# Half-size expert weight chunks, router logits taken from x, and output transposes laid between the last scatter products

## The chip, the cores and the metric

The kernel runs on one core of a Trainium2 chip, in float32. The metric is device time in microseconds (us) of one execution. Three executions of the kernel before took 1821.88, 1827.37 and 1827.48 us; the median is 1827.37 us. A separate profiled execution took 1822.55 us, and the span from its first to its last instruction was 1820.4 us.

## The reference

One inference step of a two-layer decoder for 256 prompt tokens and 8 sample tokens (264 in all, D = 1024). Each layer has a mixer, then a feed-forward part. The change lies wholly in the feed-forward part of layer 1, a top-2-of-8 mixture of experts:

```
h = rms_norm(x, norm_ffn)                       # x * rsqrt(mean(x*x)) * w
logits = einsum('btd,de->bte', h, moe_router)   # 8 experts
probs = softmax(logits); top_p, top_i = top_k(probs, 2); top_p /= sum(top_p)
hg = einsum('btd,edf->btef', h, moe_w_gate)     # F = 1792
hu = einsum('btd,edf->btef', h, moe_w_up)
a  = silu(hg) * hu * gate
x  = x + einsum('btef,efd->btd', a, moe_w_down)
```

## The kernel before

Activations lie transposed, `x[:, d, :]` being 128 features by 264 tokens, for d from 0 to 7. Each engine runs its own program; semaphores order them. SyncE (SP) issues all weight loads on one queue.

**The weights of the experts.** They are cut into 42 sets: two groups g of four experts, and 21 sets t for each group. Sets 0 to 13 hold pieces of the gate and up matrices (`GU_SETS`: 4 row blocks k by 512 columns, or in the last two 8 row blocks by 256 columns), sets 14 to 20 two row blocks of the down matrix. A set is four transfers of 1024 KB, one for each expert, so all are 168 transfers. Three sets fit on the chip at a time (set t lies in slots 4*(t%3) to 4*(t%3)+3). `load_set(n)` waits until `sets_used` says that set n-3 is used up and then issues its four transfers. Sets 1, 2 and 0 are loaded ahead, during the end of the mixer.

**The router** (`route`). After the last output product of the mixer (`wo`, d = 7) ScalarE squares x, TensorE sums the squares in PSUM bank 0, ScalarE forms `rs` (logarithm, then exponential), and VectorE's `xnorm` writes h = x * w * rs in eight steps. TensorE multiplies h by the router matrix (L1481), again into bank 0, VectorE copies the logits, TensorE turns them so that tokens are rows, and a chain of small VectorE steps finds the two experts of each token (`top`), the counts (`r_flag`) and the slot matrix G (`r_slots`). Meanwhile TensorE turns h itself to rows (`token_rows`) and ScalarE copies it to `htok`.

**The gather** (`gather_first`). Six products of no use (`WARM_R`) run once the branch is taken; then four `gather_pair` calls multiply `htok` by G, and ScalarE copies the results to `hs`, the tokens of each expert side by side.

**Hidden and down products** (`hidden_chosen`, `down_chosen`). For each set TensorE waits until all of it has landed, then works for r = 0 and 1 (32 products each, four of them side by side in the array, columns 32j) and in between two `over_piece` calls of 16 for experts with many tokens, whose weights VectorE copies out first (`bring`, L2853). The sets of gate and up are followed by `turn_hidden`. `sets_used` is raised at the first product of the next set.

**The end.** The sums of the down products lie in banks 0, 1, 4, 5 and 6; ScalarE copies them to `ys`. `scatter(1, d)` multiplies them back to tokens, for eight d, in banks 4 + d % 4; VectorE adds each to x (`add_tile`, L2823). When all are added, `give_back` turns x to rows (24 transposes in banks 0 to 5), and ScalarE copies the banks and issues the three output transfers.

## Time and profile before

| | us |
|---|---|
| median of three executions | 1827.37 |
| profiled execution | 1822.55 |
| its span | 1820.4 |
| TensorE busy | 1757.7 (97% of the span) |
| VectorE busy | 746.4 (41%) |
| ScalarE busy | 362.3 (20%) |
| first expert product; copy of the last down sum begins | 1362.61; 1800.81 |

TensorE's busy time is the time in which some product is under way; it says little on whether a product waited for anything else. Times below count from the span's start.

### The profile page before, as it was taken

The page shows a single profiled execution, that of the slowest core. Times are in us where ns is not written, and L with a number is a line of the kernel's source. Part 1 is how long each engine was busy: PE and PEld are TensorE (multiplying, and loading weights), DVE is VectorE, ACT ScalarE, POOL GpSimd, SP SyncE. Part 2 cuts the span into 40 slices and gives each one's busy share as a digit, 9 for nine tenths or more (in the row PEclk, how much of TensorE's full clock was granted, in tenths as well). Part 3 has the DMA queues.
Part 4 walks back from the last instruction along what each step waited for, and adds up shares of the span by engine and source line. Part 5 has one row for each costly group of instructions (what it writes and reads, how often), then busy time and mean ns, then how long its engine had stood idle before and what let it go on. Part 6 is the DMA issues. An engine that isn't in the chain of part 4 may idle for free.

```text
span 1820.4 us, 30085 instructions
## 1 busy us (share of the span) xinstructions
PE 1757.7 (97%) x12545; PEld 1299.3 (71%) x12545; DVE 746.4 (41%) x1551; ACT 362.3 (20%) x760; POOL 154.3 (8%) x259
## 2 busy tenths in 40 slices
...
GB/s 289 286 120 104 194 308 342 349 327 365 387 341 395 357 324 272 303 354 362 159 85 262 285 350 342 314 370 380 341 91 320 393 379 414 385 397 393 380 414 157
DMA packets 263163, 563.94 MB, mean 310 GB/s; under 512 B 11965, under 2 KB 160673, under 8 KB 262752
## 3 DMA queue, kind: packets, MB, share of 16 engines
...
## 4 chain that ended last, share of the span: by engine, by line
PE 86%; DMA 7%; SPq 3%; DVE 2%; issue 1%; ACT 1%; POOL 0%; DVEq 0%; ACTq 0%
PE PS L930 34%; PE PS L1364 8%; PE PS L1585 7%; PE PS L1340 5%; PE PS L1372 4%; PE PS L849 3%; SPq L801 3%; PE PS L1623 3%; DMA mem<-in_moe_w_up 3%; PE PS L976 3%; PE PS L1565 3%; PE PS L1354 2%; DMA z<-in_moe_w_down 2%; PE PS L969 2%; PE PS L1524 2%; PE PS L1311 1%
## 5 line engine op out<-in xcount | busy, mean ns | idle before, releaser
L930 PE MATMUL PS<-h,mem 128*128 128x264 f32 x2816 | 655.4, 389 | 0.0
L930 PEld LDWEIGHTS PS<-h,mem 128*128 128x128 f32 x2816 | 528.6, 191 | 107.0 <-issue 21.3
L1773 ACT COPY z<-PS 128x264 f32<-128x264 f32 (+6 forms) x311 | 127.5, 430 | 817.0 <-PE PS L930 528.2
L1585 PE MATMUL PS<-mem,z 128*32 128x512 f32 (+1 forms) x1536 | 148.8, 533 | 15.9 <-DMA mem<-in_moe_w_up 9.0
L1585 PEld LDWEIGHTS PS<-mem,z 128*32 128x32 f32 x1536 | 54.6, 112 | 87.5 <-issue 78.1
L2853 DVE COPY small<-mem 128x1024 f32 x56 | 38.9, 694 | 170.4 <-PE PS L1565 112.7
L1565 PE MATMUL PS<-small,z 128*32 128x256 f32 (+2 forms) x624 | 87.8, 396 | 0.0
L1340 PE MATMUL PS<-z,mem 128*128 128x264 f32 x384 | 87.3, 388 | 0.0
L1565 PE MATMUL PS<-z 128*32 128x256 f32 (+2 forms) x624 | 87.1, 397 | 0.0
L1340 PEld LDWEIGHTS PS<-z,mem 128*128 128x128 f32 x384 | 72.3, 190 | 13.8 <-issue 1.7
L1364 PE MATMUL PS<-z,mem 128*128 128x132 f32 x624 | 78.3, 278 | 0.0
L1364 PEld LDWEIGHTS PS<-z,mem 128*128 128x128 f32 x624 | 74.5, 192 | 0.0
L1565 PEld LDWEIGHTS PS<-small,z 128*32 128x32 f32 x624 | 37.0, 110 | 48.6 <-issue 40.5
L1770 ACT ACTIVATE z<-z 128x1056 f32<-128x1056 f32 (+3 forms) x54 | 56.9, 1053 | 62.3 <-DVEq L2677 54.2
L1364 PE MATMUL PS<-h,mem 128*128 128x132 f32 x488 | 63.2, 278 | 2.8 <-DVE h L2174 2.8
L1372 PE MATMUL PS<-z,mem 128*128 128x132 f32 x550 | 63.5, 276 | 0.0
L1623 PE MATMUL PS<-mem,z 128*32 128x512 f32 x512 | 58.1, 593 | 5.0 <-DMA mem<-in_moe_w_down 5.0
L1372 PEld LDWEIGHTS PS<-z,mem 128*128 128x128 f32 x550 | 62.6, 190 | 0.0
L1364 PEld LDWEIGHTS PS<-h,mem 128*128 128x128 f32 x488 | 59.2, 192 | 3.2 <-issue 3.2
L1354 PE MATMUL PS<-z,mem 128*128 128x264 f32 x256 | 59.5, 387 | 2.0 <-DVE z L2612 2.0
L1770 ACT ACTIVATE z<-x 128x264 f32<-128x264 f32 x32 | 13.1, 421 | 235.1 <-DVE x L2619 160.2
L1585 PE MATMUL PS<-z 128*32 128x512 f32 x512 | 58.0, 593 | 1.2 <-DMA z<-in_moe_w_up 1.2
...
## 6 DMA issues: line engine op xcount, KB each, us to landing
out_win_s<-in_cache_win_kv SPq DMA_DIRECT2D x128, 1023.5 KB, 11.7
...
```

Of the source, the lines that this page charges most:

```text
L801: sp.dma_start(v3(slot_ap(s_), src.shape[1]), src).then_inc(landed[s_], 16)
L849: return tr(out, in_, ident[0:rows, 0:rows])
L930: last = mm(bank(l, "p", j)[:, 0:T], w[:, k, P * (j % 2):P * (j % 2) + P], h[:, k, :], start=(k == 0), stop=(k == KT - 1))
L1340: last = mm(bank(l, "mb", b, d)[:, 0:T], v3(chunk(ch[k // 2]), 2)[:, k % 2, P * d:P * d + P], src[b][:, k, :], start=(k == 0), stop=(k == 3))
L1354: last = mm(bank(l, "wo", d)[:, 0:T], w[:, k, P * (d % 2):P * (d % 2) + P], z[:, k, :], start=(k == 0), stop=(k == KT - 1))
L1364: last = mm(out, left[:, k, :], right[:, k, :], start=(opens and k == 0), stop=(k == 3), skip_group_check=True)
L1372: last = mm(out, left[:, k, :], right, start=(opens and c == 0 and k == 0), stop=(k == DOWN_KS[c] // 2 - 1), skip_group_check=True)
L1565: last = mm(out[BLK * s_:BLK * s_ + BLK, :], tokens[:, k, QUAD * FULL + BLK * a_:QUAD * FULL + BLK * a_ + BLK], v3(over[a_], len(ks))[:, k ...
L1585: last = mm(m_bank("c", "gu", g, b, w, r)[BLK * j:BLK * j + BLK, 0:n], hs[:, k, P * r + BLK * j:P * r + BLK * j + BLK], v3(slot_ap(set_slo ...
L1623: last = mm(m_bank("c", "dn", g, n)[BLK * j:BLK * j + BLK, :], fc[:, k, P * r + BLK * j:P * r + BLK * j + BLK], v3(slot_ap(set_slot(SET_EG ...
L1770: return nc.scalar.activation(out, in_, func, **kw)
L1773: return nc.scalar.copy(out, in_)
```

## The change

It has three parts.

**Half chunks.** A set's transfer for each expert is cut in two halves by row blocks (p = 0, 1), so a set is eight transfers of 512 KB. Each half has a semaphore of its own (`half_in`), TensorE waits for a half, does the products of both r for its row blocks and one `over_piece`, and raises `sets_used` at the third last product of that piece (84 times for 42 sets). Half p of set n is loaded when half p of set n-3 is used.

**Router.** The norm weight is multiplied into the router matrix ahead of time on VectorE (`wr_w`, between tiles 4 and 5 of `wo`), and the logits are products of x, not of h, in four column groups of the array, which the constant `fold` adds up while it turns them. The factor rs of each token is turned too (three small products) and multiplied in by VectorE and by ScalarE's copies to `htok`; the norm weight is multiplied in as `hs` is copied. `xnorm(1, 1)` is gone from this path. The six products of `WARM_R` are gone. Only two of the four gather pairs come ahead of set 0; the others come behind its first and its second half.

**The end.** The scatter sums use banks 6 and 7 in place of 4 to 7. The transposes of tile d-2 stand behind the scatter products of tile d. The first two tiles' full-expert products stand ahead of the waits for the later `dn` sums.

```diff
 
-WARM, WARM_R = 12, 6
+WARM = 12
...
@@ -519,7 +520,7 @@
                 out.append((("tf", g, ROUNDS * len(BLOCKS) - 1), 2 + (ROUNDS * len(BLOCKS) - 1) % 2))
                 if g == 0:
                     out += [(("gh", 1, d), 2 + d % 2) for d in range(KT)]
-            out += [(("fd", 1, d), 4 + d % 4) for d in range(KT)]
+            out += [(("fd", 1, d), 6 + d % 2) for d in range(KT)]
             return out
 
         def tiles_of(b):
             return ztail[:, (s_ - 2 * QUAD) * CW:(s_ - 2 * QUAD + 1) * CW]
 
+        def half_in(t, p, g):
+
+            s_ = set_slot(t, p)
+            return landed[s_], 16 * loads[s_] + 16 * QUAD * ((SETS * g + t) // 3 + 1)
+
...
-                for j in range(QUAD):
-                    s_, e = set_slot(t, j), QUAD * g + j
+                for p in range(2):
                     if n >= 3:
-                        if j == 0:
-                            sp.wait_ge(sets_used, n - 2)
-                    elif s_ < RING:
-                        wait_full(sp, *held[s_])
-                    if t < SET_EG:
-                        b, w, part = GU_SETS[t]
-                        ks = slice(4 * part, 4 * part + 4) if part is not None else slice(0, KT)
-                        w_ = a["moe_w_up" if w else "moe_w_gate"][0]
-                        src = w_[e].rearrange("(k p) n -> p k n", p=P)[:, ks, BLOCKS[b][0]:sum(BLOCKS[b])]
-                    else:
-                        q = t - SET_EG
-                        src = a["moe_w_down"][0][e].rearrange("(k p) n -> p k n", p=P)[:, 2 * q:2 * q + 2, :]
-                    sp.dma_start(v3(slot_ap(s_), src.shape[1]), src).then_inc(landed[s_], 16)
+                        sp.wait_ge(sets_used, 2 * (n - 3) + p + 1)
+                    for j in range(QUAD):
+                        s_, e = set_slot(t, j), QUAD * g + j
+                        if n < 3 and p == 0 and s_ < RING:
+                            wait_full(sp, *held[s_])
+                        if t < SET_EG:
+                            b, w, part = GU_SETS[t]
+                            k0, nk = (4 * part, 2) if part is not None else (0, 4)
+                            w_ = a["moe_w_up" if w else "moe_w_gate"][0]
+                            src = w_[e].rearrange("(k p) n -> p k n", p=P)[:, k0 + nk * p:k0 + nk * p + nk,
+                                                                            BLOCKS[b][0]:sum(BLOCKS[b])]
+                        else:
+                            k0, nk = 2 * (t - SET_EG) + p, 1
+                            src = a["moe_w_down"][0][e].rearrange("(k p) n -> p k n", p=P)[:, k0:k0 + 1, :]
+                        sp.dma_start(v3(slot_ap(s_)[:, D * p:D * p + D], nk), src).then_inc(half_in(t, p, g)[0], 16)
 
             pieces = [(g, l, b, n) for l in range(DEPTH) for b in range(NS) for g in (2, 1, 0)
...
                         down_second(-m)
 
             def route():
-                pe.wait_ge(router_in, 16)
                 open_bank(pe, 1, "rl", 0)
                 for k in range(KT):
-                    pe.wait_ge(sems["h_ready"], V("h_ready", 1, 8 + k))
-                    last = mm(bank(1, "rl", 0)[0:NE, 0:T], wr[:, 8 * k:8 * k + 8], h[:, k, :],
-                              start=(k == 0), stop=(k == KT - 1))
+                    j = k % 4
+                    last = mm(bank(1, "rl", 0)[BLK * j:BLK * j + BLK, 0:T], wr_w[:, k, :], x[:, k, :],
+                              start=(k < 4), stop=(k >= 4))
                 last.then_inc(full(1, "rl", 0), 1)
+                open_bank(pe, 1, "rt", 0)
+                pe.wait_ge(sems["rs_ready"], V("rs_ready", 1, 1))
+                for i, (t0, nt) in enumerate(TOKS):
+                    mm(bank(1, "rt", 0)[0:nt, 24 + 8 * i:32 + 8 * i], rs[0:1, t0:t0 + nt], ones[0:1, 0:8],
+                       start=True, stop=True)
                 wait_read(pe, 1, "rl", 0)
-                open_bank(pe, 1, "rt", 0)
                 for i, (t0, nt) in enumerate(TOKS):
-                    last = turn_over(bank(1, "rt", 0)[0:nt, 8 * i:8 * i + 8], rlog[0:NE, t0:t0 + nt], NE)
+                    last = mm(bank(1, "rt", 0)[0:nt, 8 * i:8 * i + 8], rlog[:, t0:t0 + nt], K("fold"),
...
 
                 for n in range(2 * len(TOKS)):
                     wait_read(pe, 1, "ht", n)
-                for _ in range(WARM_R):
-                    mm(PS[:, 7, 0:T], h[:, 0, 0:P], h[:, 0, :], start=True, stop=True)
                 pe.wait_ge(r_slots, 1)
-                for d in range(0, KT, 2):
-                    gather_pair(0, d)
+                gather_pair(0, 0)
+                gather_pair(0, 2)
 
             def turn_hidden(g, u):
...
                             last.then_inc(sets_used, 1)
                 return last
...
-                    m_wait_read(pe, "c", "gh", g, d)
                 for t, (b, w, part) in enumerate(GU_SETS):
-                    set_landed(g, t)
                     n = BLOCKS[b][1]
                     ks = range(4 * part, 4 * part + 4) if part is not None else range(KT)
-                    for r in range(2):
-                        if not part:
-                            m_open(pe, "c", "gu", g, b, w, r)
-                        for k in ks:
-                            for j in range(QUAD):
-                                last = mm(m_bank("c", "gu", g, b, w, r)[BLK * j:BLK * j + BLK, 0:n],
-                                          hs[:, k, P * r + BLK * j:P * r + BLK * j + BLK],
-                                          v3(slot_ap(set_slot(t, j)), len(ks))[:, k - ks[0], :],
-                                          start=(k == 0), stop=(k == KT - 1))
-                                if (g or t) and r == 0 and k == ks[0] and j == 0:
-                                    last.then_inc(sets_used, 1)
-                        if part != 0:
-                            last.then_inc(m_done("c", "gu", g, b, w, r), 1)
-                            if w and b + r:
-                                turn_hidden(g, ROUNDS * b + r - 1)
-                        if not part and r == 0:
+                    for p in range(2):
+                        pe.wait_ge(*half_in(t, p, g))
+                        for d in range(4 * t + 2 * p, 4 * t + 2 * p + 2) if t < 2 else ():
+                            m_wait_read(pe, "c", "gh", g, d)
+                        half = ks[p * len(ks) // 2:(p + 1) * len(ks) // 2]
+                        for r in range(2):
+                            if not part and p == 0:
+                                m_open(pe, "c", "gu", g, b, w, r)
+                            for k in half:
+                                for j in range(QUAD):
+                                    last = mm(m_bank("c", "gu", g, b, w, r)[BLK * j:BLK * j + BLK, 0:n],
+                                              hs[:, k, P * r + BLK * j:P * r + BLK * j + BLK],
+                                              v3(slot_ap(set_slot(t, j)), len(ks))[:, k - ks[0], :],
+                                              start=(k == 0), stop=(k == KT - 1))
+                            if part != 0 and p == 1:
+                                last.then_inc(m_done("c", "gu", g, b, w, r), 1)
+                                if w and b + r:
+                                    turn_hidden(g, ROUNDS * b + r - 1)
+                        if not part and p == 0:
                             m_open(pe, "c", "gu", g, b, w, 2)
-                        half = ks[r * len(ks) // 2:(r + 1) * len(ks) // 2]
-                        last = over_piece(g, t, r, m_bank("c", "gu", g, b, w, 2)[:, 0:n // 2], hs, half, KT)
-                        if part != 0 and r == 1:
+                        last = over_piece(g, t, p, m_bank("c", "gu", g, b, w, 2)[:, 0:n // 2], hs, half, KT)
+                        if part != 0 and p == 1:
                             last.then_inc(m_done("c", "gu", g, b, w, 2), 1)
                         else:
                             last.then_inc(over_used, 1)
...
                         gather_pair(1, 2 * (q - 2))
 
+            def scatter_full(g, d):
+
+                m_open(pe, "c", "fd", g, d)
+                for r in range(2):
+                    mm(m_bank("c", "fd", g, d)[:, 0:T], ys[:, r, P * d:P * d + P], ST[:, QUAD * g + r, :],
+                       start=(r == 0), stop=False)
+
+            def scatter_over(g, d):
+
+                mm(m_bank("c", "fd", g, d)[:, 0:T], ys_over[:, P * (d % 4):P * (d % 4) + P], ST[:, QUAD * g + 2 + d // 4, :],
+                   start=False, stop=True).then_inc(m_done("c", "fd", g, d), 1)
+
             def scatter(g, d):
 
                 if d == 0:
                     for n in range(2 * ROUNDS - 1):
                         m_wait_read(pe, "c", "dn", g, n)
-                    for n in range(2 * QUAD) if g == 0 else ():
+                    for n in range(2 * QUAD):
                         m_wait_read(pe, "c", "st", n)
-                m_open(pe, "c", "fd", g, d)
-                out = m_bank("c", "fd", g, d)[:, 0:T]
-                for r in range(2):
-                    mm(out, ys[:, r, P * d:P * d + P], ST[:, QUAD * g + r, :], start=(r == 0), stop=False)
-                last = mm(out, ys_over[:, P * (d % 4):P * (d % 4) + P], ST[:, QUAD * g + 2 + d // 4, :],
-                          start=False, stop=True)
-                last.then_inc(m_done("c", "fd", g, d), 1)
+                scatter_full(g, d)
+                scatter_over(g, d)
+
+            def turn_y(d):
+
+                for i, (t0, nt) in enumerate(TOKS):
+                    last = turn_over(PS[0:nt, 2 * i + d // 4, P * (d % 4):P * (d % 4) + P], x[:, d, t0:t0 + nt], P)
+                    if d % 4 == 3:
+                        last.then_inc(y_full, 1)
+
+            def scatter_last():
+
+                for n in (0, 2):
+                    m_wait_read(pe, "c", "dn", 1, n)
+                scatter_full(1, 0)
+                scatter_full(1, 1)
+                for n in (1, 3, 4):
+                    m_wait_read(pe, "c", "dn", 1, n)
+                scatter_over(1, 0)
+                scatter_over(1, 1)
+                for d in range(2, KT):
+                    scatter(1, d)
+                    m_wait_read(pe, "c", "fd", 1, d - 2)
+                    turn_y(d - 2)
+                for d in range(KT - 2, KT):
+                    m_wait_read(pe, "c", "fd", 1, d)
+                    turn_y(d)
 
             def experts_chosen():
...
-                copy(htok[n // 2][0:nt, 512 * (n % 2):512 * (n % 2) + 512], bank(1, "ht", n)[0:nt, :]).then_inc(
-                    free(1, "ht", n), 1)
+                if n == 0:
+                    wait_read(act, 1, "rt", 0)
+                act_(htok[n // 2][0:nt, 512 * (n % 2):512 * (n % 2) + 512], bank(1, "ht", n)[0:nt, :], ACT.Copy,
...
-                    copy(hs[:, d, :], m_bank("c", "gh", g, d)[:, 0:SLOTS]).then_inc(m_read("c", "gh", g, d), 1)
+                    act_(hs[:, d, :], m_bank("c", "gh", g, d)[:, 0:SLOTS], ACT.Copy,
+                         scale=wnf[:, d:d + 1]).then_inc(m_read("c", "gh", g, d), 1)
 
...
+                    if l == 1 and d == 4:
+                        dve.wait_ge(router_in, 16)
+                        cp(wnf, par[:, R_NF:R_NF + KT])
+                        link(nc.vector.memset(wr_w, 0.0))
+                        link(tt(wr_w[:, :, 0:NE], v3(wr, KT), bc(par[:, R_NF:R_NF + KT], 2, [P, KT, NE]), MUL))
 
...
                     n = 2 * (SETS * g + t) + p
-                    if p == 0:
-                        for j in range(QUAD):
-                            s_ = set_slot(t, j)
-                            dve.wait_ge(landed[s_], 16 * (loads[s_] + (SETS * g + t) // 3 + 1))
+                    dve.wait_ge(*half_in(t, p, g))
...
+                        bring(g, t, 1)
                         if up:
                             gate_up(g, ROUNDS * b)
-                        bring(g, t, 1)
-                        if up:
                             gate_up(g, ROUNDS * b + 1)
                         if g and 2 <= t < 10:
                             add_tile("c", 0, t - 2)
```

The first place is TensorE's program between the mixer's last product and the first expert products. Before (L864 sums squares, L1481 makes the logits, L849 turns, L1534 is `WARM_R`, L1524 the gather):

```order
L864 MATMUL PS<-z,con 128x264 x2
L1481 MATMUL PS<-h,mem 8x264 x8
L849 MATMUL PS<-con,z 128x8 x2
L849 MATMUL PS<-con,z 8x8
L849 MATMUL PS<-con,h 128x128 x16
...
L1727 TENSOR_LOAD crowded
L1727 ISA x2
L1728 COMPARE_AND_BRANCH
L1534 MATMUL PS<-h 128x264 x6
L1524 MATMUL PS<-mem 128x320 x4
L1524 MATMUL PS<-mem,z 128x320 x2
```

After (L874 sums squares, L1490 makes the logits, L1496 turns rs, L1500 turns the logits, L859 turns x, L1537 is the gather, L1598 are expert products):

```order
L874 MATMUL PS<-z,con 128x264 x2
L1490 MATMUL PS<-x,z 32x264 x8
L1496 MATMUL PS<-con,small 128x8 x2
L1496 MATMUL PS<-con,small 8x8
L1500 MATMUL PS<-con,z 128x8 x2
L1500 MATMUL PS<-con,z 8x8
L859 MATMUL PS<-con,x 128x128 x16
...
L1761 COMPARE_AND_BRANCH
L1537 MATMUL PS<-mem 128x320 x4
...
L1537 MATMUL PS<-mem 128x320 x4
L1537 MATMUL PS<-mem,z 128x320 x2
L1598 MATMUL PS<-mem,z 32x512 x16
```

The logits now read x and a 32-column matrix, the turns read x, the six products from h are gone, and expert products follow two gather pairs.

The second place is SP's queue where the loads begin to wait for used sets. Before:

```order
L801 DMA mem<-in_moe_w_gate 128x4x512 [waits bank_full3]
L801 DMA mem<-in_moe_w_up 128x4x512 [waits sets_used]
L801 DMA mem<-in_moe_w_up 128x4x512 x3
L801 DMA mem<-in_moe_w_gate 128x4x512 [waits sets_used]
L801 DMA mem<-in_moe_w_gate 128x4x512 x3
```

After:

```order
L811 DMA mem<-in_moe_w_gate 128x2x512 [waits bank_full3]
L811 DMA mem<-in_moe_w_gate 128x2x512 x4
L811 DMA mem<-in_moe_w_up 128x2x512 [waits sets_used]
L811 DMA mem<-in_moe_w_up 128x2x512 x3
L811 DMA mem<-in_moe_w_up 128x2x512 [waits sets_used]
```

Each wait now stands ahead of four transfers of half the size.

The third place is TensorE's end, behind the last `over_piece`. Before (L1652 and L1653 scatter):

```order
L1565 MATMUL PS<-z 32x512 x2
L1652 MATMUL PS<-h,z 128x264 x2
L1653 MATMUL PS<-h,z 128x264
L1652 MATMUL PS<-h,z 128x264 x2
L1653 MATMUL PS<-h,z 128x264
```

After (L1657 and L1662 scatter, L859 turns x), with what each waits for:

```order
L1576 MATMUL PS<-z 32x512 x2
L1657 MATMUL PS<-h,z 128x264 [waits bank_free6,bank_free4,bank_free0]
L1657 MATMUL PS<-h,z 128x264
L1657 MATMUL PS<-h,z 128x264 [waits bank_free7]
L1657 MATMUL PS<-h,z 128x264
L1662 MATMUL PS<-h,z 128x264 [waits bank_free6,bank_free5,bank_free1]
L1662 MATMUL PS<-h,z 128x264
L1657 MATMUL PS<-h,z 128x264 [waits bank_free6]
L1657 MATMUL PS<-h,z 128x264
L1662 MATMUL PS<-h,z 128x264
L859 MATMUL PS<-con,x 128x128 [waits bank_free6]
```

The first scatter product still waits for bank 6, which holds the last of the down sums, and a turn of x now follows each tile from the third on.

## Rows read from the trace of the kernel before

**Rows 1.** Windows: length, busy us by engine, granted clock, DMA share, GB/s

```profile
1362.00:1380.00 18.00, 17.39 (x196) 7.74 (x200) 3.90 (x6) 2.40 (x3) 0.00 (x0) 1.00 0.37 132
1380.00:1400.00 20.00, 19.23 (x205) 7.65 (x197) 7.82 (x13) 1.94 (x4) 0.00 (x0) 1.00 1.05 391
...
1700.00:1720.00 20.00, 16.20 (x270) 9.67 (x266) 5.59 (x9) 2.76 (x7) 0.00 (x0) 1.00 1.09 354
...
1740.00:1760.00 20.00, 19.27 (x183) 6.21 (x177) 5.18 (x8) 0.27 (x1) 0.00 (x0) 1.00 1.03 415
```

**Rows 2.** Timeline of SP's queue: start, us, the issues

```profile
1309.62 14.33 SPq L801 DMA_DIRECT2D mem<-in_moe_w_gate  x4
1372.25 2.28 SPq L801 DMA_DIRECT2D mem<-in_moe_w_up  x4
...
1770.38 5.49 SPq L801 DMA_DIRECT2D z<-in_moe_w_down  x4
```

**Rows 3.** The chain that ended last, from the gather on: start, us, what

```profile
1346.95 14.50 PE PS L1524 x48
1362.61 3.64 PE PS L1585 x32
1366.25 0.86 PE PS L1565 x16
...
1773.52 18.20 DMA z<-in_moe_w_down
```

**Rows 4.** Waits of TensorE from 1310 us on: total us, times, longest

```profile
PE PS L1585 <- DMA mem<-in_moe_w_up: 9.0, 4, 3.1
...
PE PS L1585 <- DMA z<-in_moe_w_up: 1.2, 1, 1.2
```

**Rows 5.** Timeline of the router stage: start, us, instructions, idle before and releaser

```profile
1325.28 0.39 ACT L1770 ACTIVATE small<-PS 128x264 f32<-128x264 f32 x1 [0.80 <-PE PS L864]
...
1326.87 5.33 PE L1481 MATMUL PS<-h,mem 128*8 128x264 f32 x16 [1.63 <-DVE h L2174]
...
1333.40 0.18 DVE L2739 TENSOR_REDUCE z<-z 128x3 f32<-128x24 f32 x1
...
1339.15 0.13 DVE L2772 TENSOR_SCALAR crowded<-z 1x1 int32<-1x1 f32 x1
...
1341.10 0.36 DVE L2800 TENSOR_TENSOR mem<-con,z 128x192 f32<-128x192 f32 x1
...
1341.34 5.62 PE L1534 MATMUL PS<-h 128*128 128x264 f32 x12 [2.41 <-issue]
...
1354.87 0.69 DVE L2853 COPY z<-mem 128x1024 f32 x1
```

**Rows 6.** TensorE by 1 us windows: busy us, granted clock, DMA share, GB/s

```profile
1345.00:1346.00 1.00, 1.00 (x4) 0.50 0.00 0
...
1348.00:1349.00 1.00, 1.00 (x5) 1.00 0.00 0
```

**Rows 7.** DMA from 1720 to 1780 us: 24 transfers of 1024 KB

```profile
DMA packets 6453, 24.89 MB, mean 415 GB/s; under 512 B 375, under 2 KB 401, under 8 KB 6447
...
q1 hardware_dynamic: 6447, 24.79, 102.0%
```

**Rows 8.** Window with small transfers among the others, columns as in rows 1

```profile
1220.00:1240.00 20.00, 19.28 (x90) 14.48 (x89) 13.86 (x25) 5.09 (x7) 4.83 (x9) 1.00 1.03 393
```

**Rows 9.** DMA issues from 1180 to 1250 us: count, KB each, us to landing

```profile
mem<-in_cache_win_kv POOLq DMA_DIRECT2D x18, 256.0 KB, 9.6
```

**Rows 10.** Timeline of the end

```profile
1801.65 1.13 PE L1652 MATMUL PS<-h,z 128*128 128x264 f32 x4 [0.89 <-ACT z L1773]
...
1812.61 0.43 DVE L2823 TENSOR_TENSOR x<-x,PS 128x264 f32<-128x264 f32 x1 [0.91 <-PE PS L1653]
...
1813.85 1.07 ACT L1773 COPY z<-PS 128x512 f32<-128x512 f32 x2 [12.45 <-PE PS L849]
...
1817.93 0.54 ACTq L2138 DMA_DIRECT2D out_y_sample<-z  x1
```

70 lines of the change are left out of this document (35 added, 35 removed).

## The prediction

> **What bounds the kernel now.** The page says 97% for TensorE, so the windows come first. From 1380 us on they show the DMA share at 1.02 to 1.09 in every stretch, at 391 GB/s with packets of 2 KB, 415 with 4 KB, and 354 where the 256-column blocks make them 1 KB [rows 1]. Only 1362 to 1380 us is different: share 0.37. The queue's timeline says why: the three sets loaded ahead were issued by 1324 us, and the fourth set, which needs the slots of set 0, at 1372.25 us. After that SP never pauses until the last set, issued from 1770.38 us [rows 2], which lands at 1791.7 us (1773.52 + 18.20) [rows 3]. So 39 sets take 1791.7 - 1372.25 = 419.5 us, 10.75 us each, and a set costs TensorE 2 x (3.43 + 0.86) = 8.6 us, the distance at which such pieces follow each other (3.64 us, of which the next overlaps 0.2, and 0.86) [rows 3]. TensorE's waits for DMA in this stage are in five rows with a sum of 22.7 us (the largest and the smallest stand there) [rows 4]. They look small because TensorE began with three sets in hand and, in the first group's down part, had gather work to do while the DMA caught up. The end is nevertheless the DMA's: last landing, then 8.6 us of products, then the tail.
>
> So I ask of each edit how much sooner it makes **the queue restart**, and what stands behind **the last landing**.
>
> **Router.** Before, the logits' products start at 1326.87 us, held by h, and run 5.33 us; the maximum that opens VectorE's chain comes at 1333.40 [rows 5]. After, they need only x and bank 0, whose sum of squares ScalarE reads until 1325.28 + 0.39 = 1325.7. Eight products in four column groups: as 16 instructions of `over_piece` (256 columns) they take 0.86 us [rows 3], or 1.7 at half clock. With 0.3 us to drain they end at 1327.0 to 1327.8, against 1332.2. From there to the maximum it was 1.2 us, and VectorE now has two copies and two multiplications for two copies, +0.35. The maximum comes at 1328.6 to 1329.4; I take 1329.0, **4.4 us earlier**. Preparing `wr_w` (three small steps after tile 4 of `wo`) lies in pauses of 3.6 us between VectorE's additions, and costs 0.8 us at most if that cover failed. ScalarE's copies of `htok` now wait for rs in rows, about 0.3 us ahead of the maximum; they are done some 5 us later, ahead of G.
>
> **Gather.** G is ready at 1341.10 + 0.36 = 1341.46 us, but the six useless products stand before it from 1341.34, and the gather starts at 1346.95 [rows 3, 5]. Without them it starts at 1341.46 - 4.4 = 1337.1, 9.85 us earlier. Those six ran at granted clock 0.50, the gather's later ones at 1.00 [rows 6]. TensorE has stood idle ahead of them by 2.41 us [rows 5], as it will again, so the low clock falls on the gather: two pairs take half of 14.50, 7.25 us, plus 2.8 if the low level lasts as long as those products' 5.6 us. Bounds: 0 (clock stays up) and 7.25. With 2.8, set 0 starts at 1347.1 in place of 1362.61.
>
> **Restart.** Set 0's first half: 3.43 us of products, to 1350.5; its `over_piece` needs VectorE's copy, which ended at 1354.87 + 0.69 = 1355.56 [rows 5] and so now at 1351.2. TensorE waits 0.7 us and ends the half at 1352.1. Before, from the end of set 0's products (1371.2) to the issue 1.05 us passed: the first half load goes at 1353.1. Then a gather pair (3.6) and a half (4.3): second release at 1360.0, issue 1361.1; again both: 1367.9, issue 1369.0; from then a half is released each 4.3 us and needs 5.35 to load, so the queue is never empty. That equals an unbroken start at 1369.0 - 2 x 5.35 = 1358.3: **13.9 us earlier** than 1372.25. Would TensorE be late later? Its own work, with all waits for DMA gone and the earlier start, would end near 1800.8 - 22.7 - 9.85 + 2.8, 1771 us: some 12 us ahead of the data. It stays behind the DMA.
>
> **After the last landing.** The half that lands last has 4.3 us of products in place of 8.6: **4.3 us**.
>
> **Price of half transfers.** 156 more transfers. In 1720 to 1780 us there are 375 packets under 512 B for 24 transfers, about 16 each, one for each engine [rows 7]. 1 MB takes 2.53 us at 415 GB/s and 2.68 at 391, with 16 more packets per engine: 9 ns for a packet. At that price 156 transfers cost 1.4 us. Upper bound: in 1220 to 1240 us, with 256 KB loads going on, 393 GB/s flow [rows 8], where packets of 2 and 4 KB should give some 403 between them. In 1180 to 1250 us there are two rows of 18 such loads [rows 9], about 10 in 20 us; 2.5% of 20 us over 10 is 0.05 us each, 8 us for 156. That stretch also carries cache copies from memory to memory, which may be the whole deficit, so I take near the lower: **-2 us**.
>
> The Trainium skill speaks against the halving: DMA: Bandwidth & Descriptors, section Bandwidth, asks to batch to 1 MiB or more for 75% of peak, and its Anatomy of one DMA gives some 2 us fixed for each. By that, paid one after the other, 156 transfers would add 312 us. The trace contradicts it in this form: with 2 us and the bytes, 1 MB would run at about 240 GB/s, and it runs at 415, because several are in flight.
>
> SP's 8 issues for a set cost 8 x 0.37 to 0.6, under 5 us of 10.7.
>
> **The end.** Bank 6 holds the fifth down sum, and the first scatter product waits for its copy as before, so it starts as before (1801.65 us [rows 10]); the early full-expert products gain nothing. Each tile takes 1.335 us. With two banks, tile 2 waits some 0.3 us once for the addition of tile 0; afterwards a turn (2.81/8 = 0.35) stands between and covers it. Five turns stand ahead of tile 7, so the last addition, before at 1812.61 + 0.43, ends 2.0 us later. Then only three transposes, three copies and two issues follow (about 2.7 us) in place of 24 transposes and the chain 1813.85 to 1817.93 (4.1 and 0.8 before it). Sum: **0**, bounds -0.7 and +1.
>
> **Sum.** 13.9 + 4.3 - 2 + 0 = 16.2 us. On the profiled execution, 1822.55 - 16.2 = 1806.4; the median before lies 4.8 higher, 1827.37 - 16.2 = 1811.2. I say **1810**. What moves it: gather clock +2.8/-4.4, router 0.4, price of transfers +0.6/-6, tail 1.
>
> **Rivals.**
> *The halves cost more at the engines.* At 0.03 to 0.12 us each the gain is 13 down to nothing. For it: the bound of 0.05 [rows 8, 9], which is for transfers mixed with others. Against: 16 packets in 272 are little, and the share is already 1.02 in time of packets. At 0.06: 18.2 - 9.4, 1818.5.
> *It ends slower.* The same mechanism past 18.2/156 = 0.117 us a transfer is break-even, and 0.152 gives slower by 5.5 us; at 0.2 us, 1827.4 + 13 = 1840. It must then hold that the engines stop at each transfer's end, which an even 415 GB/s speaks against. The batching rule of the Trainium skill points this way.
> *TensorE was the bound, or DMA runs faster when never held back.* Then the earlier start and the absent waits count: 1827.4 - 30, 1797. Against: share 1.02 to 1.09 without a gap.
> *The release does not come earlier*, because something I hold for covered (VectorE's first copy, banks of the gather) keeps set 0 until about 1368: only half of a set and the last half count, minus 2, about 1821 to 1827: no change.
>
> **How the numbers follow.** This kernel's measurement tells 0.3%, 5.5 us, from no change. Forecast (1804 to 1816): 0.62. Dearer halves: 0.2, of which 0.15 faster and 0.05 within 0.3%. Slower: 0.05. TensorE-bound or faster DMA: 0.08. Release not earlier: 0.05, same. Faster 0.62 + 0.15 + 0.08 = 0.85, same 0.10, slower 0.05. The range takes in half of the dear and the fast cases: 1802 to 1820.
>
> **What would show it.** Right: SP's first load behind set 0 near 1353 us and three spaced issues; share above 1.0 from 1369 us on; last landing near 1779; then 4.3 us to the last product; the gather's first products at clock 0.50; the end's stretch from the last down sum to the end of span 19.6 us as before. Wrong: GB/s under 385 (2 KB) or 405 (4 KB) in the steady part, or TensorE without waits for DMA in the second group.

## The result, and the profile after

| | before | after |
|---|---|---|
| median, us (four executions each) | 1825.39 (1821.88 to 1827.48) | 1804.95 (1804.16 to 1810.43) |
| profiled execution, us | 1822.55 | 1804.24 |
| its span, us | 1820.4 | 1802.1 |

The ratio is 0.9896, 95% interval 0.9869 to 0.9924: 19 to 20 us faster. The prediction said 1810 in a range of 1802 to 1820. What follows compares the profiled executions, 18.3 us apart.

The same windows as in [rows 1] (length, busy us of TensorE, its weight loads, VectorE, ScalarE and GpSimd, granted clock, DMA share, GB/s):

```profile
1362.00:1380.00 18.00, 18.00 (x184) 6.42 (x186) 3.88 (x6) 3.53 (x5) 0.00 (x0) 1.00 0.89 321
1380.00:1400.00 20.00, 19.23 (x206) 7.30 (x202) 6.89 (x11) 2.31 (x5) 0.00 (x0) 1.00 1.05 401
...
1740.00:1760.00 20.00, 17.96 (x164) 4.78 (x160) 5.18 (x8) 0.00 (x0) 0.00 (x0) 1.00 1.03 415
```

The hole of share 0.37 between 1362 and 1380 us is gone, and the rates of the full queue are no lower than with 1 MB transfers (401 and 415 GB/s against 391 and 415). SP's queue, as in [rows 2]:

```profile
1312.20 14.00 SPq L811 DMA_DIRECT2D mem<-in_moe_w_gate  x8
1352.07 9.97 SPq L811 DMA_DIRECT2D mem<-in_moe_w_up  x8
1368.19 6.20 SPq L811 DMA_DIRECT2D mem<-in_moe_w_gate  x8
...
1752.06 10.16 SPq L811 DMA_DIRECT2D z<-in_moe_w_down  x8
```

The restart is at 1352.07 us, with the first half of set 3 (sets count from 0, so this is the fourth set of the prediction). The first half of set 4 goes at 1368.19, which is the third release that the prediction put at 1369.0. Two halves of 5.35 us back give an unbroken start at 1357.5, against 1372.25 before: 14.75 us. The router and the gather, as in [rows 5] and [rows 3]:

```profile
1325.71 1.10 PE L1490 MATMUL PS<-x,z 128*32 128x264 f32 x16 [0.48 <-ACT small L1803]
...
1328.82 0.18 DVE L2782 TENSOR_REDUCE z<-z 128x3 f32<-128x24 f32 x1
...
1337.27 3.92 PE L1537 MATMUL PS<-mem 128*128 128x320 f32 x8 [2.57 <-DVEq L2845]
...
1346.01 3.64 PE L1598 MATMUL PS<-mem,z 128*32 128x512 f32 x32
...
1350.13 0.69 DVE L2893 COPY z<-mem 128x1024 f32 x1
1350.97 0.41 PE L1576 MATMUL PS<-small,z 128*32 128x256 f32 x2 [1.32 <-DVE z L2893]
```

The clock in the same stretch (length, TensorE busy, granted clock, DMA share, GB/s), as in [rows 6]; 1.00 is 2.4 GHz and 0.50 is 1.2 GHz:

```profile
1332.00:1336.00 4.00, 2.35 (x18) 0.69 0.05 13
1336.00:1340.00 4.00, 2.73 (x5) 0.50 0.01 4
1340.00:1344.00 4.00, 4.00 (x14) 0.95 0.00 0
```

TensorE's waits from 1310 us on (total us, times, longest), as in [rows 4]:

```profile
PE PS L1636 <- DMA mem<-in_moe_w_down: 6.7, 12, 1.0
PE PS L1598 <- DMA mem<-in_moe_w_up: 3.8, 2, 2.2
```

And the end: first the last landing from the chain of waits, then the timeline, as in [rows 10]:

```profile
1761.15 15.70 DMA z<-in_moe_w_down
```

```profile
1776.89 3.64 PE L1636 MATMUL PS<-z 128*32 128x512 f32 x32 [0.42 <-DMA z<-in_moe_w_down]
1782.22 2.02 PE L1657 MATMUL PS<-h,z 128*128 128x264 f32 x8 [0.82 <-ACT z L1806]
...
1795.17 0.43 DVE L2866 TENSOR_TENSOR x<-x,PS 128x264 f32<-128x264 f32 x1 [1.24 <-PE PS L1662]
...
1797.66 0.60 ACTq L2174 DMA_DIRECT2D out_y_prompt<-z  x1
1798.91 0.53 ACTq L2174 DMA_DIRECT2D out_y_sample<-z  x1
```

The last half lands at 1776.85 us and TensorE starts on it 0.04 us later: the DMA is what ends last, as before.

### The profile page after: what moved, and what is told of

Its sections match the earlier page's. It is cut to its first block, busy times and chain, and to the rows that moved or that the text cites. A ratio compares the mean times of both kernels' runs of the same rounds, so it can differ in the third digit from the quotient of the medians.

```text
span 1802.1 us, 30183 instructions
## 1 busy us (share of the span) xinstructions
PE 1748.8 (97%) x12542; PEld 1282.9 (71%) x12542; DVE 743.5 (41%) x1548; ACT 364.3 (20%) x760; POOL 154.3 (9%) x259
## 3 DMA queue, kind: packets, MB, share of 16 engines
q8 instruction: 102, 1.67, 0.4%
## 4 chain that ended last, share of the span: by engine, by line
PE 85%; SPq 7%; DMA 4%; DVE 2%; issue 1%; ACT 1%; DVEq 0%; POOL 0%; ACTq 0%; POOLq 0%
PE PS L940 34%; PE PS L1598 8%; PE PS L1374 8%; SPq L811 7%; PE PS L1350 5%; PE PS L1382 4%; PE PS L859 3%; PE PS L986 3%; PE PS L1576 3%; PE PS L1364 2%; PE PS L979 2%; PE PS L1636 2%; PE PS L1321 1%; PE PS L1537 1%; DMA mem<-bias_tables 1%
## 5 line engine op out<-in xcount | busy, mean ns | idle before, releaser
L1806 ACT COPY z<-PS 128x264 f32<-128x264 f32 (+5 forms) x293 | 119.5, 430 | 737.6 <-PE PS L940 527.6
L1598 PE MATMUL PS<-mem,z 128*32 128x512 f32 (+1 forms) x1536 | 146.1, 523 | 3.8 <-DMA mem<-in_moe_w_up 3.8
L1598 PEld LDWEIGHTS PS<-mem,z 128*32 128x32 f32 x1536 | 47.4, 110 | 77.8 <-issue 61.2
L1598 PE MATMUL PS<-z 128*32 128x512 f32 x512 | 58.4, 593 | 0.0
```

The lines of the kernel that those rows point to most:

```text
L1598: last = mm(m_bank("c", "gu", g, b, w, r)[BLK * j:BLK * j + BLK, 0:n], hs[:, k, P * r + BLK * j:P * r + BLK * j + BLK], v3(slot_ap(set_slo ...
L1806: return nc.scalar.copy(out, in_)
```

## The experiments

All are edits of the changed kernel. Each ratio below is to the kernel before, executed beside the edited one. Its medians there were 1820.17 to 1820.95 us, and 1825.39 beside the changed kernel, so kernels are compared by ratio and not by time. The stages ahead of the router end up to 8 us apart in these profiles, whatever stands behind them, so each profile is read in four pieces that don't contain that: from the start of the logits' products (L) to the queue's restart, from there to set 4's first issue, from that to the first scatter product, and from that to the end of the span. For the kernel before, L is 1325.7 us, where the changed kernel's logits could start. The last column says for how long the granted clock stood at 0.50 from the router's idle time on. Each row is one profiled execution. Some of the later expectations call set 4, whose issue the table gives, "the fourth set".

| us | L at | to restart | to set 4 | to scatter | to end | sum | clock low for |
|---|---|---|---|---|---|---|---|
| before | 1325.7 | 46.6 | 8.6 | 420.8 | 18.8 | 494.7 | ~7 |
| after | 1325.7 | 26.4 | 16.1 | 414.0 | 19.9 | 476.4 | ~7 |
| late_release | 1321.4 | 41.1 | 12.4 | 413.8 | 19.9 | 487.1 | ~24 |
| whole_landing | 1321.6 | 33.0 | 16.1 | 418.5 | 19.7 | 487.4 | ~24 |
| gather_ahead | 1325.2 | 32.4 | 8.6 | 417.6 | 19.7 | 478.4 | ~7 |
| skip_products | 1325.6 | 32.8 | 16.1 | 413.3 | 20.1 | 482.3 | ~20 |
| whole_chunks | 1321.7 | 51.8 | 8.6 | 420.9 | 20.1 | 501.3 | ~31 |
| quarters | 1326.7 | 26.4 | 16.1 | 415.0 | 19.8 | 477.2 | ~7 |
| old_tail | 1325.6 | 33.0 | 16.1 | 414.0 | 18.8 | 481.9 | ~24 |
| warm_back | 1323.4 | 27.3 | 16.1 | 413.9 | 19.8 | 477.2 | ~7 |
| keep_clock | 1327.4 | 26.4 | 16.1 | 413.0 | 19.9 | 475.4 | 0 |
| early_copy | 1322.8 | 23.3 | 16.1 | 413.0 | 19.6 | 472.0 | 0 |
| early_release | 1323.0 | 23.3 | 8.6 | 421.1 | 19.8 | 472.9 | 0 |
| early_both | 1329.7 | 23.3 | 16.1 | 413.2 | 18.8 | 471.4 | 0 |

### Is the time from restart to landing the DMA's? (skip_products)

```diff
-                                for j in range(QUAD):
+                                for j in range(QUAD) if r == 0 or b not in (1, 2) or k in (0, KT - 1) else ():
```

> The changed kernel, but in the sets of the second and third column block (8 sets of each group) three quarters of the products of r = 1 are left out, 2.57 us of TensorE's work for each of 16 sets, 41 us in all; the sums of those rows are incomplete, all transfers are the same. My theory (DMA-bound from 1368 us on): last landing and span unchanged within 1 us, 1802. Rival (TensorE-bound in part): the span falls by up to 17 us. TensorE may drop to half clock in its longer pauses; by my theory that costs nothing unless it happens in the last half.

Measured: median 1812.06 us of 5, ratio 0.9948 (0.9930 to 0.9966). SP's queue:

```profile
1358.36 9.95 SPq L811 DMA_DIRECT2D mem<-in_moe_w_up  x8
1374.45 6.20 SPq L811 DMA_DIRECT2D mem<-in_moe_w_gate  x8
```

From set 4's issue to the last landing (1782.38) 407.9 us pass, against 408.7 in the changed kernel, with 41 us of TensorE's work taken out of that stretch. The clock fell again in TensorE's longer pauses (granted clock 0.87 between 1436 and 1444 us, 0.79 between 1456 and 1464), and the DMA share stayed at 1.05 and 1.06 there. The stretch is the DMA's; that TensorE bounds it is refuted. The span was not the forecast's 1802 but 1807.8 us, since the restart lay 6.4 us later behind L. That is the clock, below.

### Half waits and half releases, one at a time (late_release, whole_landing)

```diff
-                        sp.wait_ge(sets_used, 2 * (n - 3) + p + 1)
+                        sp.wait_ge(sets_used, 2 * (n - 3) + 2)
```

> The changed kernel, but SP loads both halves of set n only when both halves of set n-3 are used. My theory (the end is the DMA's, set by when its queue restarts without a gap): both halves of the fourth set go at about 1360 us in place of 1352 and some 1359, the fifth set's when set 1 is used, about 1372, so the unbroken start moves from 1357.5 to about 1361.9, and the span grows by 4.4 us over the 1802.1 of the changed kernel, to 1806.5. Rival (TensorE's own work is the bound): no change, since TensorE has three sets in hand: 1802.

In the second, TensorE waits for both halves of a set before the first one's products:

```diff
                     for p in range(2):
-                        pe.wait_ge(*half_in(t, p, g))
+                        pe.wait_ge(*half_in(t, 0, g))
+                        pe.wait_ge(*half_in(t, 1, g))
```

> The changed kernel, but TensorE starts no half of a set before both have landed. My theory: the loads and releases of the first sets stay where they are, and only the last set counts: 8.6 us of products behind the last landing in place of 4.3, so the span is 1802.1 + 4.3 = 1806.4. Rival (waits for data are not at the end but all along): each of the 39 sets loses part of its 5.3 us, and the span grows by much more than 4.3 us. Rival (TensorE-bound): 0.

Measured: late_release 1807.58 us (4 executions, ratio 0.9917, 0.9893 to 0.9942) and whole_landing 1811.29 us (8, 0.9935, 0.9917 to 0.9954). In late_release both halves of a set go together:

```profile
1362.47 4.05 SPq L811 DMA_DIRECT2D mem<-in_moe_w_up  x8
1374.82 5.81 SPq L811 DMA_DIRECT2D mem<-in_moe_w_gate  x8
```

Both profiles have the long stretch of low clock, as have skip_products and old_tail, whose sums are 482.3 and 481.9 (483.0 with the changed kernel's end, which is 1.1 us longer than old_tail's). Against skip_products late_release is 4.8 us longer, and whole_landing 5.1 us; against old_tail, put right for its end, 4.1 and 4.4. In whole_landing nearly all of it lies between set 4's issue and the scatter (418.5 against 413.3): the second half of the last set has its 4.3 us of products, and the first half its own, behind the last landing. Each of the two is worth about a half's time; 4.4 and 4.3 us were forecast. In late_release nearly all of it is the later unbroken start: set 4's issue less 10.7 us is 42.8 us behind L, against 38.2 in skip_products.

### The half chunks alone undone (whole_chunks)

Loads, waits, the gather's place and VectorE's order are the old ones, and a set is released whole; the logits from x and the new end stay.

```diff
-                for p in range(2):
+                for j in range(QUAD):
+                    s_, e = set_slot(t, j), QUAD * g + j
                     if n >= 3:
-                        sp.wait_ge(sets_used, 2 * (n - 3) + p + 1)
+                        if j == 0:
+                            sp.wait_ge(sets_used, n - 2)
```

> The half chunks alone are undone: sets are loaded in pieces of 1 MB, waited for and released whole, all four gather pairs stand ahead of set 0, VectorE's copies in the order of the kernel before. The logits from x and the laid-in output turns stay. Theory (the end follows the start of the unbroken queue and the products behind the last landing): against the kernel before, the gather starts 9.7 us earlier by the logits (1337.3 against 1346.95); all four pairs take 14.5 us at full clock, about 16 with the short stretch at 0.50; set 0's products and release as before, so the restart comes at about 1364.0 in place of 1372.25, 8.2 us earlier; behind the last landing a whole set's 8.6 us of products; tail 0.8 us longer. Span 1820.4 - 8.2 + 0.8 = 1813, some 11 us above the changed kernel's 1802.1 (about 6.5 from the restart, 4.3 from the last landing); with the long stretch at 0.50 some 5 to 7 us more. Rival: whole megabyte transfers are cheaper than halves, by 2 us or more over the 419 us of the queue; then restart to last landing is under 417 us here, and the span under 1811. Rival: the logits alone gave nothing, since the queue bound them: then 1820.

Measured: median 1818.98 us of 12 (1811.62 to 1827.40), ratio 0.9986 (0.9967 to 1.0004). The gather in its profile, as in [rows 3]:

```profile
1333.65 4.61 PE L1537 MATMUL PS<-mem 128*128 128x320 f32 x8 [2.66 <-DVEq L2845]
1338.18 2.50 PE L1537 MATMUL PS<-mem,z 8*128 8x320 f32 x4
...
1354.60 4.64 PE L1537 MATMUL PS<-mem 128*128 128x320 f32 x8
```

A gather pair takes 7 us in place of 3.6. The clock is back at 1.00 only from 1360 us on and falls again in the first products of set 0 (0.68 between 1362 and 1366). So the restart is 51.8 us behind L, 5.2 later than in the kernel before, although the gather itself starts 9.3 us earlier. The forecast span of 1813 is a time of about 1815. Five of the twelve executions come to it (1811.62 to 1815.99, mean clock 0.991 to 0.993); the other seven took 1818.70 to 1827.40 at a mean clock of 0.984 to 0.989. So without the halves the logits' gain shows where the clock is high, and is lost to the clock in the others. That the two groups are the short and the long stretch of low clock is argued from the mean clock; only the profiled execution has a trace. The last load lands here:

```profile
1774.29 18.82 DMA z<-in_moe_w_down
```

From the restart (1373.48) to this landing (1793.11) it is 419.6 us, against 419.35 from the unbroken start with halves: a discount for whole megabytes is not seen.

### The price of a transfer (quarters)

```diff
+                        if t < SET_EG and n > 2:
+                            for i in range(2):
+                                sp.dma_start(v3(slot_ap(s_)[:, D * p + D // 2 * i:D * p + D // 2 * i + D // 2], nk // 2),
+                                             src[:, nk // 2 * i:nk // 2 * i + nk // 2]).then_inc(half_in(t, p, g)[0], 16)
```

> Every load of a gate or up set behind the first three is cut once more, into two transfers of 256 KB on the same semaphore; what TensorE, VectorE and SyncE wait for, and the size of the packets, stay. So the gate and up sets have nearly twice as many transfers, about 200 more over both groups of experts. Theory: the price of a transfer in the full queue is at most a hundredth of a microsecond or nothing, as the step from 1 MB to 512 KB showed (419.5 us from unbroken start to last landing before, 419.35 after): from the fourth set's first issue to the last landing 408 to 410 us, span as the changed kernel's for its clock pattern (1802 or 1808). Rival: 0.05 us each: then +8 to +10 us, about 418 us from that issue to the last landing. Rival: SyncE issues one transfer per about 0.78 to 1.24 us, and a transfer of 256 KB takes 0.65 us at 400 GB/s: the issuing engine becomes the bound in the gate and up sets, the queue runs dry there and the stretch grows by 20 us or more.

Measured: median 1802.94 us of 6, ratio 0.9899 (0.9881 to 0.9917). SP issues sixteen for a set, still in time:

```profile
1353.01 11.86 SPq L814 DMA_DIRECT2D mem<-in_moe_w_up  x16
1369.13 9.27 SPq L814 DMA_DIRECT2D mem<-in_moe_w_gate  x16
```

200 more transfers made set 4's issue to the scatter 1.0 us longer, 0.005 us each, which is no more than these stretches differ among the others. Both rivals fall. The Trainium skill (DMA: Bandwidth & Descriptors, section Bandwidth) advises to batch to 1 MiB or more. This trace doesn't bear that out for a queue that is kept full: here 256 KB do as well. In this run TensorE's waits and releases stayed those of halves, so it says what a transfer costs, and not what a finer release would gain.

### The place of the gather (gather_ahead)

```diff
-                gather_pair(0, 0)
-                gather_pair(0, 2)
+                for d in range(0, KT, 2):
+                    gather_pair(0, d)
```

> The changed kernel with all four gather pairs ahead of set 0, as before. The first load behind set 0 then goes some 5.5 us later (about 1357.6 in place of 1352.1), but the third half, which started the unbroken stretch, some 2 us earlier. My theory, by which the end follows the latest of (start of half k minus k loads of 5.36 us): 1357.6 in place of 1357.5, so no change, 1802 within 1 us. Rival (the end follows the first load behind set 0): 5.5 us later, 1807.6.

Measured: median 1807.28 us of 10 (1802.40 to 1822.55), ratio 0.9936 (0.9911 to 0.9961). The restart comes 6.0 us later behind L, but the next issues then follow without gaps (8.6 us to set 4 in place of 16.1), and 2.0 us of the sum remain: so much is the later place of two gather pairs worth. No change within 1 us was forecast. Of the 2.0, 0.6 is the unbroken start, 32.4 us behind L here and 26.4 + 16.1 - 10.7 = 31.8 in the changed kernel. The rest lies behind it, where the DMA share was not yet full; what else it is stays open:

```profile
1362.00:1364.00 2.00, 2.00 (x24) 0.65 (x20) 1.30 (x2) 0.00 (x0) 0.00 (x0) 1.00 0.78 218
```

The rival's 5.5 us is refuted.

### The end (old_tail)

The last scatter's sums stand in four banks again and all turns behind the last of them.

```diff
-            out += [(("fd", 1, d), 6 + d % 2) for d in range(KT)]
+            out += [(("fd", 1, d), 4 + d % 4) for d in range(KT)]
...
-                scatter_last()
+                for d in range(KT):
+                    scatter(1, d)
```

> The third part of the change is undone alone: the last scatter's sums stand in four banks, and the output's eight turns all come behind the last scatter product, as in the kernel before; half chunks and the logits from x stay. Theory: the start of the last scatter to the end of the execution took 18.75 us in the kernel before and 19.9 us in the changed kernel's profile, 0.7 us of that difference in the final transfer, 0.4 in the chain ahead of it; so undoing it gives 0.4 to 1.1 us back at the end: scatter to end about 18.8 to 19.5 us. Rival: the interleaved order does save something, hidden by the final transfer's own scatter; then scatter start to the issue of the last output is over 16.7 us here, and the end is the same or up to 1 us later. The time as a whole is set by the queue's restart as in the changed kernel, 1804 to 1811 by the clock in the router stage.

Measured: median 1806.42 us of 5, ratio 0.9921 (0.9907 to 0.9934), with the long stretch of low clock in its profile. Its end:

```profile
1788.74 1.13 PE L1657 MATMUL PS<-h,z 128*128 128x264 f32 x4 [1.09 <-issue]
...
1799.69 0.43 DVE L2877 TENSOR_TENSOR x<-x,PS 128x264 f32<-128x264 f32 x1 [0.91 <-PE PS L1662]
...
1803.55 0.34 ACTq L2185 DMA_DIRECT2D out_y_prompt<-z  x1
1805.02 0.54 ACTq L2185 DMA_DIRECT2D out_y_sample<-z  x1
```

Tiles follow each other at 1.33 us here and at 1.67 with two banks. From the first scatter product to the last issue it is 16.3 us, against 16.7; from that issue to the end 2.5, against 3.2, where the issues stand 1.25 us apart and not 1.5. Counted from the start of the last 32 down products the end takes 24.4 us (1783.14 to 1807.5) against 25.2, so the change's third part costs 0.8 us in these profiles; early_both below, with the same end, repeats the 18.8. By the medians (ratio 0.9921 against 0.9896, intervals overlapping) it can't be seen.

### The clock (warm_back, keep_clock)

Five of the eight profiles of kernels without added products show the clock at 0.50 through the gather, with no edit ahead of it. In whole_landing, for one:

```profile
1340.00:1344.00 4.00, 4.00 (x8) 0.50 0.00 0
1344.00:1348.00 4.00, 4.00 (x10) 0.50 0.01 2
1352.00:1356.00 4.00, 4.00 (x34) 0.89 0.11 11
```

The first test puts the six useless products back:

```diff
+                for _ in range(6):
+                    mm(PS[:, 7, 0:T], x[:, 0, 0:P], x[:, 0, :], start=True, stop=True)
                 pe.wait_ge(r_slots, 1)
```

> The six useless products that the kernel before had in front of the gather are put back, and nothing else; all the rest is the changed kernel. In the changed kernel's profile the clock was granted at 0.50 from about 1332 to 1340 us, and the gather began at 1337.3; in three of the edited kernels it stayed at 0.50 for some 20 us, through the whole gather, and the queue's restart came about 6.5 us later. Theory: those six products (about 5.6 us at the low clock) make the gather begin at about 1342.9, but at full clock: pairs of 7.25 us for the first two, set 0 at about 1350.2, first half of it read out about 2.5 us later than in the changed kernel's profile, restart at about 1354.5 in place of 1352.1, span about 1804.5, and no execution with the long stretch at 0.50, so that the times lie closer together (about 1806 to 1808). Rival: the long stretch comes whatever stands before the gather; then there are executions near 1813, and the low clock reaches past 1350 in some profile. Rival: the six products cost their whole 5.6 us on the end, so that the span is 1807.7.

The second puts eight where TensorE was idle anyway:

```diff
                     token_rows(n)
+                fill(3)
                 pe.wait_ge(r_mask, 1)
...
                 last.then_inc(full(1, "rp", 0), 1)
+                fill(5)
```

> Eight useless products fill TensorE's idle time in the router stage of the changed kernel: three behind the token turns, ahead of its wait for the mask, five behind the rank products, ahead of its wait for the branch. In the changed kernel's profile TensorE was idle there (about 1331 to 1332.3 and 1334.8 to 1337.2 us), so they move nothing by themselves. Theory: with the idle time filled the clock is back at full when the gather begins or soon after; the gather's first two pairs take 7.25 us, set 0 begins at about 1344.6, but the first over piece still waits for VectorE's copy, which ended at 1350.8 in the changed kernel, so the restart of the queue stays at about 1352 and the span at about 1802 to 1803. What goes is the long stretch at 0.50 (restart 6.5 us later) of three of the edited kernels, and with it the spread: all executions at 1804 to 1806. Rival: the clock falls all the same, since these few products are not enough to bring it back; then restarts at about 1358 and times near 1811 appear too.

Measured: warm_back 1801.82 us (4 executions, 1799.33 to 1803.20; ratio 0.9896, 0.9879 to 0.9913) and keep_clock 1804.12 us (5, 1800.57 to 1805.19; 0.9905, 0.9890 to 0.9921). None of these nine came to the 1809 to 1812 that the kernels without such products show, nor did the 14 executions of the three kernels of the next section, which have the eight products too (at most 1803.78). The mean clock of all 23 was 0.992 to 0.997; the five profiles with the long stretch have 0.984 to 0.988. By the ratio neither kernel can be told from the changed one (0.9896). Nearly all executions lie below the forecasts (1806 to 1808 and 1804 to 1806), and they spread by 4 to 5 us still, since L does. In keep_clock the clock never fell in this stage (three windows of its profile):

```profile
1334.00:1336.00 2.00, 1.93 (x19) 1.00 0.03 8
1336.00:1338.00 2.00, 2.00 (x11) 1.00 0.00 0
1338.00:1340.00 2.00, 1.41 (x7) 1.00 0.02 4
```

As expected, its restart stayed at 26.4 us behind L, since VectorE's copy holds it (1.3 us of waiting before, now 2.8):

```profile
PE PS L1583 <- DVE z L2900: 2.8, 1, 2.8
```

The early_copy expectation below puts that wait at 6 us; it counts from the start of set 0 and leaves out the 3.6 us of its first products. In warm_back the clock fell too (0.50 between 1332 and 1336 us) but was back before the gather, which begins here:

```profile
1338.95 2.32 PE L1537 MATMUL PS<-mem 128*128 128x320 f32 x8
```

The six delayed the gather by 4.0 us (15.6 behind L, against 11.6), not 5.6, but the restart by only 0.9, less than the 2.4 expected: the gather ran at full clock (1.5 us), and the wait of 1.3 us for the copy is gone. So taking the six out, which was a part of the change, gained 0.8 us of the sum where the clock came back early (476.4 against 477.2). Where it did not, the sum is about 483.0 (old_tail's with the changed end), so that it cost nearly 6 us.

### Moving that copy, and what then binds (early_copy, early_release, early_both)

With the idle time filled as in keep_clock, VectorE makes its first copy before its work on the second group's slots:

```diff
-                find_slots(1)
-                for g in range(2):
-                    weigh_slots(g)
...
                 bring(0, 0, 0)
+                find_slots(1)
+                for g in range(2):
+                    weigh_slots(g)
```

> The filled idle time of the kernel with eight useless products, and beside it VectorE's first copy of gathered rows moved ahead of its work on the slots of the second group (find slots, weigh slots), which only later stages need. Theory: in the changed kernel's profile TensorE waited 1.3 us for that copy ahead of set 0's second over piece; with the clock up, the wait would be about 6 us (set 0 at 1344.6, copy ended at 1350.8). Moved forward, the copy is done when the gather's second pair ends, so that the first half of set 0 is read out at about 1348.9, every release of a half comes about 3 us earlier, the unbroken queue begins at about 1354.5 in place of 1357.5, and the span is about 1799. This is the same arithmetic as my explanation of the change: a microsecond earlier at the restart is a microsecond at the end. Rival: the restart is bound by the later sets, not by the first (the fourth set's issue follows the third's products), and moves by less than 1 us; then the span is that of the kernel without this move, about 1802. Rival: the low clock stays, span 1808.

Measured: median 1798.81 us of 5 (1796.87 to 1803.78), ratio 0.9889 (0.9873 to 0.9906). The copies now end at 1339.61, and the restart follows:

```profile
1338.92 0.69 DVE L2897 COPY z<-mem 128x1024 f32 x1
```

```profile
1346.12 9.96 SPq L811 DMA_DIRECT2D mem<-in_moe_w_up  x8
1362.23 6.51 SPq L811 DMA_DIRECT2D mem<-in_moe_w_gate  x8
```

The restart is 3.1 us earlier behind L than in keep_clock, the sum 3.4. Nothing was touched at the queue or behind it. A microsecond at the restart is a microsecond at the end. (The rest of this profile's distance to keep_clock's is L itself, 4.6 us apart.)

The next kernel adds another order of the sets:

```diff
-GU_SETS = [(b, w, part) for b in range(3) for w in range(2) for part in range(2)] + [(3, 0, None), (3, 1, None)]
+GU_SETS = [(b, w, part) for b in range(3) for part in range(2) for w in range(2)] + [(3, 0, None), (3, 1, None)]
...
-                        if g == 0 and t == 0:
-                            gather_pair(0, 4 + 2 * p)
+                        if g == 0 and (t, p) in ((1, 1), (2, 0)):
+                            gather_pair(0, 4 + 2 * (t - 1))
```

> On top of the filled idle time, VectorE's earlier first copy and the tail of the kernel before, the sets of a block come as gate first half, up first half, gate second, up second, not gate, gate, up, up. So the first two sets need only the first four gathered tiles; the gather's third and fourth pair stand behind set 1 and behind set 2's first half, not inside set 0. (The branch for crowded experts, which these inputs never take, isn't adapted to this order.) Theory: with the earlier copy alone, logits' products to restart took 23.3 us, and restart to the fourth set's first issue 16.1, of which the full queue needs 10.7: 5.4 us were lost to gaps between the first releases, each half of set 0 having a gather pair of 3.6 us behind it. Without these TensorE frees halves faster than the DMAs fill them, and the fourth set's first issue comes 3.5 to 5.4 us earlier (34.0 to 36 us behind the logits' products, not 39.4). With 0.85 us of the tail the span is 4.3 to 6.2 us below the kernel with the earlier copy, for the same time of the logits: 1789 to 1791 if they come at 1322.8, 1793 at 1326. Rival: the gather pairs now delay set 2's products, and the queue is held there: no gain at the fourth set's issue. Rival: the first transfers of a restarted queue are slow in themselves: a gap of 5 us stays at any order.

Other than the expectation says, the kernel that ran had the changed kernel's end and not the old one, so its span was to be 0.85 us longer than stated there. Measured: median 1798.22 us of 4, ratio 0.9873 (0.9853 to 0.9893), its sum 0.9 us longer than early_copy's. First two windows of early_copy, then the same and a later one of early_release:

```profile
1351.00:1355.00 4.00, 4.00 (x44) 1.00 0.58 218
1359.00:1363.00 4.00, 4.00 (x52) 1.00 0.56 209
```

```profile
1351.00:1355.00 4.00, 4.00 (x48) 1.00 1.02 369
1359.00:1363.00 4.00, 3.74 (x16) 1.00 1.05 387
1376.00:1380.00 4.00, 4.00 (x47) 1.00 0.54 168
```

The holes between the first releases are closed, and set 4's issue comes 7.5 us earlier, more than the 3.5 to 5.4 forecast; then the share falls to 0.54 at 1376 us, and from set 4's issue to the scatter it takes 8.1 us longer. So the forecast gain of the span didn't come. The rival named first is right in its cause, not in its sign: there was a gain at set 4's issue, but the hold moved behind it. Where it moved to, set 2, whose release waits for the gather pairs, is argued from the order of the products.

Last, early_copy with the end of old_tail:

> The two edits that helped are put together: the kernel with the filled idle time and VectorE's first copy moved ahead (23.3 us from the logits' products to the queue's restart, 1794.8 us of span), and the last scatter and output turns of the kernel before (20.7 us from the start of the last product in front of the scatter's end to the end of the execution, against 21.6 with the laid-in turns). Theory: the two parts act at different ends of the queue and add up. The logits to the restart stay at 23.3 us, the fourth set's first issue to the first scatter at about 413 us, the first scatter to the end falls from 19.6 to 18.8 us; span 1794.0 if the logits come at 1322.8 us, 1797 if at 1325.7. No long stretch at the low clock. Median 1797 to 1799. Rival: the tail's 0.85 us came from the other clock pattern in that kernel's profile and not from the order of the turns; then the first scatter to the end is again 19.6 us.

Measured: median 1798.79 us of 5 (1795.71 to 1803.11), ratio 0.9876 (0.9853 to 0.9898). Its profiled execution is a late one by L (1329.7), but all pieces are as forecast: 23.3, 16.1, 413.2, and 18.8 for the end. By its sum, 471.4 us, it is the fastest of all, 5.0 us ahead of the changed kernel; the medians tell it neither from the kernels with the same idle time filled nor, by the ratio (0.9876 against 0.9896, intervals overlapping), from the changed kernel.

## Why the prediction was right

**What bounds it.** Right: 39 sets took 419.5 us from an unbroken start to the last landing before, and 1776.85 - 1357.5 = 419.35 after; in skip_products 41 us less of TensorE's work made set 4's issue to the last landing 0.8 us shorter.

**Router and gather.** The maximum was forecast for 1329.0 and came at 1328.82; the gather for 1337.1, came at 1337.27.

**Clock.** The low level was to fall on the gather for 2.8 us. In the profiled execution it cost 1.5 (1346.01 - 1337.27 less 7.25). But other executions pay nearly the bound of 7.25: in skip_products the two pairs take 13.95 us, 6.7 more than at full clock, and set 0's first products 6.38 in place of 3.64, which the bound left out. Its restart and old_tail's, whose code up to there is the changed kernel's, come 6.4 to 6.7 us later. The changed kernel's fourth execution, 1810.43 us at a mean clock of 0.988 against 0.993, fits that; it has no trace. The forecast of 1810 was nearer to that case than to the profiled one; which of the two the median shows is luck of the executions.

**Restart.** 13.9 us forecast, 14.75 measured, but not by the terms of the sum. The clock let set 0 start 1.1 us earlier than forecast (1346.01, not 1347.1). Nearly all of that went into the wait for VectorE's copy (1.32 us, not 0.7), so that the half ended at 1351.97, only 0.1 us before the forecast's 1352.1, where TensorE goes on with the third gather pair:

```profile
1351.97 2.42 PE L1537 MATMUL PS<-mem 128*128 128x320 f32 x8
```

The rest is the issue, 0.1 us behind that end (1352.07) where the prediction kept the 1.05 us of before. It had overlooked that the change raises `sets_used` within the piece, at its third last product, and no longer at the next set's first. The next two releases took 16.1 us, not 15.9, and gave 0.2 back.

**After the last landing.** 4.3 us forecast, 4.35 measured. From the first product of the last half to the first scatter product it is 5.33 us (1776.89 to 1782.22). Before, from that of the last set, it was 9.68 (to 1801.65):

```profile
1791.97 3.64 PE L1623 MATMUL PS<-z 128*32 128x512 f32 x32 [0.85 <-DMA z<-in_moe_w_down]
```

**Price of half transfers.** This term was mis-sized: 2 us forecast, about 0.1 us the other way measured, and 0.005 us for each of the 200 of quarters. The 9 ns that it was worked out from would be 1.4 us and can't be told from none.

**The end.** 0 forecast with bounds -0.7 and +1; it cost 1.1 us in the profiled execution, 0.8 by the experiment. The tiles went as forecast: each takes 1.67 us in place of 1.335, a turn more, and the last addition ended 13.4 us behind the first scatter product (1795.60), against 11.4 before, the 2.0 later that the prediction has. What failed stands behind it. From the last addition to the last issue it took 3.3 us (1795.60 to 1798.91) in place of "about 2.7", against 4.9 before. And from the last issue to the end it took 3.2 us against 2.5, a term that the sum doesn't have. The issues stand closer together there; that this is the reason is not shown.

Together: 14.75 for the unbroken start, 0.1 for the queue, 0.2 since TensorE starts 0.04 us behind the last landing and not 0.25, 4.35 and -1.1 make the 18.3 us. The sum of 16.2 was near in part because two misses offset each other, the price put 2.1 us too high and the end 1.1 too low. 1810 then started from a median before of 1827.37, which a fourth execution moved to 1825.39.

**Rivals.** Dearer halves and the slower case: refuted by quarters. TensorE as the bound: refuted by skip_products; its 1797 was not reached. A release that doesn't come earlier: refuted by the restart, though VectorE's copy, which this rival names, does hold the first release, and in whole_chunks, without the halves and at the low clock, the restart was no earlier.
